# Output projection as one level of Strassen over pairs of token tiles, and split sums of squares

## The reference, cut to what matters

```
mod = silu(c) W_ada + b_ada -> (shift, scale, gate)
h   = rms_norm(x, g_pre) * (1 + scale) + shift
proj = h W_in                       # 1024 x 6144: q f i hg | dq dk dv dg | ma mb
o_a = hgrn2 recurrence over f, q, i (4 heads of 128), per-head rms_norm, * silu(hg)
o_b = differential attention (4 heads of 128, two maps), per-head rms_norm, * silu(dg)
y   = sigmoid(ma) * (o_a W_a) + sigmoid(mb) * (o_b W_b)
y   = y W_out                       # 1024 x 1024, "output projection"
out = x + gate * rms_norm(y, g_post)
```

## Time and profile before

| | |
|---|---|
| three runs, median | 907.11 us (904.93 to 907.34) |
| profiled execution | 902.09 us |
| its span, first to last instruction | 900.3 us |
| TensorE (PE) busy | 852.6 us, 95% |
| DVE / ACT / POOL busy | 567.0 / 450.0 / 446.2 us |
| share of PE in the chain that ended last | 80% |
| mean granted TensorE clock | 0.990 of full speed |

### The profile page before, as it was taken

One profiled execution on the slowest core, in us unless ns is written; L12 is line 12 of the kernel. 1 busy time (PEld: TensorE's weight loads), 2 busy tenths in 40 slices (PEclk: granted clock), 3 DMA queues, 4 the chain that ended last, 5 costly groups with the idle time before them and its releaser, 6 DMA issues.

```text
span 900.3 us, 12969 instructions
## 1 busy us (share of the span) xinstructions
PE 852.6 (95%) x4829; PEld 671.8 (75%) x4829; DVE 567.0 (63%) x682; ACT 450.0 (50%) x826; POOL 446.2 (50%) x336
## 2 busy tenths in 40 slices
PE   2899899999999999999999999999999999899996
PEld 2677677777777777777777777778788888678885
DVE  4889984788694897866887948746200622872222
ACT  7686222885345875336864436754445731421111
POOL 6065665455554445653554645567788461830000
PEclk9899899999999999999999999999999999999998
DMA  9914221102110120121021011102221741111331
GB/s 328 332 44 146 71 71 47 48 1 71 48 48 24 48 71 1 48 71 42 6 72 48 13 59 48 61 11 67 86 60 48 280 148 40 35 59 47 107 104 70
DMA packets 74625, 68.10 MB, mean 76 GB/s; under 512 B 3716, under 2 KB 65220, under 8 KB 74564
## 3 DMA queue, kind: packets, MB, share of 16 engines
q1 hardware_dynamic: 74448, 67.25, 23.2%
q10 hardware_dynamic: 116, 0.03, 0.0%
HBM read 58.88 MB, written 8.39 MB: 75 GB/s over the span
## 4 chain that ended last, share of the span: by engine, by line
PE 80%; DVE 11%; issue 5%; ACT 2%; SPq 1%; DMA 1%; DVEq 0%; ACTq 0%
PE pj L890 14%; PE pj L892 13%; PE pj L891 13%; PE sp L955 8%; PE sp L710 4%; PE by L725 3%; PE by L751 2%; DVE acc L1403 2%; PE sp L927 2%; PE bx L719 2%; PE sp L929 2%; PE sp L928 2%; DVE k L1537 1%; DVE sc L1578 1%; DVE q L1536 1%
## 5 line engine op out<-in xcount | busy, mean ns | idle before, releaser
L599 POOL TENSOR_TENSOR w_lo<-w_raw,w_hi 128x512 fp32r<-128x512 f32 x140 | 193.3, 1382 | 255.6 <-ACT w_hi L1169 254.1
L890 PE MATMUL pj<-b_hi,w_hi 128*128 128x512 f32 x616 | 262.0, 425 | 4.6 <-DVE dk L1517 3.3
L892 PE MATMUL pj<-b_hi,w_lo 128*128 128x512 f32 x616 | 242.2, 393 | 0.0
L891 PE MATMUL pj<-b_lo,w_hi 128*128 128x512 f32 x616 | 241.8, 393 | 0.0
L890 PEld LDWEIGHTS pj<-b_hi,w_hi 128*128 128x128 f32 x616 | 116.4, 189 | 42.1 <-issue 9.0
L892 PEld LDWEIGHTS pj<-b_hi,w_lo 128*128 128x128 f32 x616 | 116.2, 189 | 26.2
L891 PEld LDWEIGHTS pj<-b_lo,w_hi 128*128 128x128 f32 x616 | 116.7, 190 | 21.9 <-issue 3.1
L1169 ACT ACTIVATE w_hi<-w_raw 128x512 fp32r<-128x512 f32 x132 | 82.8, 627 | 63.4 <-PE pj L892 57.4
L580 POOL TENSOR_TENSOR w_raw<-w_raw,w_raw 128x512 f32<-128x512 f32 x66 | 92.7, 1404 | 3.8 <-DMA w_raw<-in_w_in 0.9
L684 POOL TENSOR_TENSOR y2n<-y2n,res 128x512 f32<-128x512 f32 x1 | 1.3, 1260 | 96.6 <-DVE y2n L1752 96.6
L1184 ACT ACTIVATE p<-sp,cols 128x1024 f32<-128x1024 f32 (+7 forms) x64 | 46.9, 738 | 0.8
(11 more groups left out here) (274 smaller groups left out, 1777.8 us busy)
## 6 DMA issues: line engine op xcount, KB each, us to landing
w_raw<-in_w_in SPq DMA_DIRECT2D x96, 256.0 KB, 4.2
x_in<-in_x SPq DMA_DIRECT2D x8, 512.0 KB, 7.1
ada<-in_w_ada SPq DMA_DIRECT2D x16, 256.0 KB, 7.1
ada<-in_w_ada SPq DMA_DIRECT2D x8, 512.0 KB, 8.1
ada_g<-in_w_ada SPq DMA_DIRECT2D x8, 512.0 KB, 3.9
wo_raw<-in_w_out SPq DMA_DIRECT2D x8, 512.0 KB, 4.2
res<-in_x SPq DMA_DIRECT2D x8, 512.0 KB, 4.1
out_x<-y2n SPq DMA_DIRECT2D x7, 512.0 KB, 2.9
```

The source lines that it names most:

```text
L599: pool.tensor_tensor(w_lo[slot(v)][:, :], raw[:, :], w_hi[slot(v)][:, :].bitcast(F32), ALU.subtract).then_inc(s_wlo, 1)
L890: pe.matmul(bank[:, :], wh, part(b_hi[m], kk), start=(fresh and kk == 0), stop=False, skip_group_check=True)
L891: pe.matmul(bank[:, :], wh, part(b_lo[m], kk), start=False, stop=False, skip_group_check=True)
L892: last = pe.matmul(bank[:, :], wl, part(b_hi[m], kk), start=False, stop=(kk == 3), skip_group_check=True)
```

## The change

**Output projection.** W_out is cut into four quarters, y into blocks of 512 rows by 128 tokens. Token tiles t and t+4 form a pair, and each of the four pairs is one more Strassen group (products `STEPS` to `END`), run by the same `product`, `snap` and `event` code and the same `pj` banks and `w_hi`/`w_lo` ring: 7 x 12 = 84 matmuls a pair where two tiles took 96. The y blocks take the place of the weights, so ACT writes a hi (`y_high`) and POOL a lo (`low_y`) for every product, and POOL makes five sums a pair (`combine_y`). The seven combinations of W_out (128x2048 each) are made by DVE (`combine_w`), split by ACT (`sum_high`) and DVE (`low_w`): those of M1, M5, M6 and M2 in the branch stage, those of M7, M3 and M4 after it. `wo_hi`, `wo_lo`, `y_hi` and `y_lo` of before are gone. Results go to SBUF (`rows_o`), one tile pair at a time; ACT squares them there, and DVE scales and adds there (`finish_o`).

**Sums of squares.** After the square ACT writes its rounded part (`hi_a`, `hi_b`) and DVE the remainder (`lo_a` in slots 60 and 61, `lo_b` in slots 33 and 48); the ones are rounded too (`ones_r`); TensorE adds two fp32r matmuls instead of one float32 one.

```diff
+LOWB_AT, LOWA_AT = (33, 48), (60, 61)
...
             sp_.wait_ge(s_olo[0], HEADS)
+            load_wo(0, b_raw[M1], 0, 0)
             for m in range(2, 2 * KT):
                 load_wb(m)
...
+            def low_y(v, raw):
+                ring_free(v)
+                pool.wait_ge(s_whj, act_highs(v) + 1)
+                pool.tensor_tensor(in_four(w_lo[slot(v)][:, :]), raw, in_four(w_hi[slot(v)][:, :].bitcast(F32)),
+                                   ALU.subtract).then_inc(s_wlo, 1)
...
+            first_sum_y(0)
+            for t in range(PAIRS_OUT):
+                a11, a12, a21, a22 = [y_tile(j, kh, t) for j in range(2) for kh in range(2)]
+                v = use(STEPS + PROD * t)
+                low_y(v + M1, a11)
+                low_y(v + M2, a12)
+                if t == 0:
+                    second_sum_y(0)
+                pool.wait_ge(s_wlo, v + M6)
+                combine_y(a11, s2, a11, ALU.add)
+                low_y(v + M6, s2)
+                combine_y(a12, a12, a22, ALU.subtract)
+                low_y(v + M5, a11)
+                low_y(v + M7, a21)
+                combine_y(a12, a12, a21, ALU.add)
+                low_y(v + M3, a12)
+                low_y(v + M4, a22)
+                if t + 1 < PAIRS_OUT:
+                    first_sum_y(t + 1)
+                    second_sum_y(t + 1)
...
                 elif name == "ssa":
-                    pe.wait_ge(s_sqa, 2 * h + n + 1)
-                    last = pe.matmul(by[:, :], ones[:, :], k[:, n * HALF:(n + 1) * HALF], start=True, stop=True)
+                    pe.wait_ge(s_loa, 2 * h + n + 1)
+                    pe.wait_ge(s_ones, 1)
+                    pe.matmul(by[:, :], ones_r[:, :], hi_a[n][:, :], start=True, stop=False)
+                    last = pe.matmul(by[:, :], ones_r[:, :], lo_a[n][:, :], start=False, stop=True)
                 elif name == "ssb":
-                    pe.wait_ge(s_sqb, 2 * h + n + 1)
...
+                    pe.wait_ge(s_lob, 2 * h + n + 1)
+                    pe.matmul(bx[:, :], ones_r[:, :], hi_b[n][:, :], start=True, stop=False)
+                    last = pe.matmul(bx[:, :], ones_r[:, :], lo_b[n][:, :], start=False, stop=True)
...
-            for t in range(NT - 1):
-                if t >= 2:
-                    pe.wait_ge(s_y2f, t - 1)
...
+            for n in range(STEPS, END):
+                for half in range(2):
+                    product(n, half)
...
                     act.activation(part(k, e), part(k, e), ACT.Square, scale=DOWN).then_inc(s_sqa, 1)
+                    act.wait_ge(s_sqa, 2 * h + e + 1)
+                    act.wait_ge(s_unit["o"], 2 * h + 2)
+                    act.activation(hi_a[e][:, :], part(k, e), ACT.Copy).then_inc(s_hia, 1)
...
+                for h, e in attention(m, LOWB_AT):
+                    dve.wait_ge(s_hib, 2 * h + e + 1)
+                    dve.tensor_tensor(lo_b[e][:, :], (sig, p1)[e][:, 0:HALF], hi_b[e][:, :].bitcast(F32),
+                                      ALU.subtract).then_inc(s_lob, 1)
...
+            def finish_o(i):
+                t, j = divmod(i, 2)
+                o = rows_o[t % 2][j][:, :]
+                norm_o(i)
+                dve.scalar_tensor_tensor(out=o, in0=o, scalar=r_o[:, i:i + 1], in1=gp_row[:, :],
+                                         op0=ALU.mult, op1=ALU.mult).then_inc(s_y2f, 1)
+                dve.wait_ge(s_y2f, i + 1)
+                dve.wait_ge(s_xr[i % 4], 16 * (i // 4 + 1))
+                dve.tensor_tensor(o, o, res[i % 4][:, :], ALU.add).then_inc(s_fin, 1)
+
+            dve.wait_ge(s_unit["br"], 4 * KT)
+            combine_w(M7, wo_22, wo_12, s_t3)
+            low_w(M3, wo_22, 1)
+            for n in range(STEPS + 1, END):
+                t, x = divmod(n - STEPS, PROD)
+                event(n - 1)
+                if t == 0 and x == 2:
+                    dve.wait_ge(s_t3, 2)
+                    low_w(M7, b_raw[M7], 2)
+                    low_w(M4, b_raw[M4], 2)
+                if t and x == 1:
+                    finish_o(2 * t - 1)
+                if x == PROD - 1:
+                    finish_o(2 * t)
...
```

More of the change, by code:

```diff
@@ L393, in build @@
         s_ysum = sem("s_ysum")
[L394 to L398, removed]
+        s_wo = [sem(f"s_wo{n}") for n in range(4)]
         s_agl = [sem(f"s_agl{n}") for n in range(4)]
@@ L409, in build @@
         s_y2f = sem("s_y2f")
-        s_xr = [sem(f"s_xr{n}") for n in range(2)]
+        s_xr = [sem(f"s_xr{n}") for n in range(4)]
         s_fin, s_finp = sem("s_fin"), sem("s_finp")
@@ L1721, in _ @@
                     dve.wait_ge(s_bro, n + 1)
[L1722 to L1729 removed]
+                    dve.tensor_tensor(part(sb[m], half), part(y[m], half), part(sb[m], half), ALU.add).then_inc(s_ysum, 1)
+                if n == 6:
+                    dve.wait_ge(s_olo[1], HEADS)
+                    dve.wait_ge(s_wo[0], 16)
+                    dve.wait_ge(s_wo[1], 16)
+                    combine_w(M5, wo_12, b_raw[M1], s_t1)
@@ L1749, in _ @@
-            norm_o(NT - 1)
-            dve.wait_ge(s_out[1], 16 * (NT // 2 - 1))
-            for n in range(2):
-                dve.scalar_tensor_tensor(out=part(y2n[1], n), in0=sp[:, 1, n * HALF:(n + 1) * HALF],
-                                         scalar=r_o[:, NT - 1:NT], in1=part(gp_row, n), op0=ALU.mult,
-                                         op1=ALU.mult).then_inc(s_y2f, 1)
+                    dve.wait_ge(s_y2s, i + 1)
+                then(dve.tensor_scalar(ss_o[:, i:i + 1], ss_o[:, i:i + 1], RS / D, EPS * RS, ALU.mult, ALU.add))
@@ L1755, in _ @@
+            norm_o(NT - 1)
+            last = rows_o[1][1]
+            for n, src in enumerate((pj[(END - 1) % 2][:, :], part(last, 1))):
+                dve.scalar_tensor_tensor(out=part(last, n), in0=src, scalar=r_o[:, NT - 1:NT], in1=part(gp_row, n),
+                                         op0=ALU.mult, op1=ALU.mult).then_inc(s_y2f, 1)
             dve.wait_ge(s_y2f, NT + 1)
-            dve.wait_ge(s_xr[1], 16 * NT // 2)
-            dve.tensor_tensor(part(y2n[1], 1), part(y2n[1], 1), part(res[1], 1), ALU.add).then_inc(s_fin, 1)
+            dve.wait_ge(s_xr[3], 32)
@@ L1760 @@
+            dve.tensor_tensor(part(last, 1), part(last, 1), part(res[3], 1), ALU.add).then_inc(s_fin, 1)
 _INS = ["x", "c", "w_ada", "b_ada", "g_pre", "g_post", "w_in", "lb_logits", "hg_norm_gain", "lambda_q1", "lambda_k1",
```

310 lines of the change are left out of this document (187 added, 123 removed).

## The result

The changed kernel is slower: 924.91 us median (919.68 to 927.00) against 906.02 us (901.99 to 907.34), ratio 1.0215 with a 95% interval of 1.0185 to 1.0245. The prediction was 910.8, with a range up to 917: the direction was right, the size was not. The profiled execution took 919.68 us with a span of 917.7, 17.4 us more than the span of 900.3 before.

The account below looks back on a forecast made before the run. TensorE was taken to bound the kernel. Sums of squares +7.8, branch stage -5.0, output stage -1.0 and tail +1.9 gave +3.7 us on a median of 907.1, so 910.8 us; range 901.5 to 917.

Parts of the forecast that it names:

- What bounds the kernel: Whole kernel: TensorE, 80% of the chain; every microsecond of it saved or stalled counts nearly in full.
- Savings on TensorE, -10.9 and -6.5: Output projection 336 matmuls instead of 384, 10.9 us less; sixteen sums of squares 0.41 each, 6.5 us, if all stayed fed.
- Sums of squares, +7.8: Rounds: TensorE waits for remainders in DVE's order, +7.8 us where 6.5 was to be gained; bounds +4 to +12.
- The first `ssb`: Rounds 1 to 3: remainder behind L1581, 1.35 us late, 0.41 saved, +0.94 each, +2.8 in all.
- The second `ssb`: Rounds 1 to 3: remainder behind L1581 delays matmul and `kt`, +1.2 us each, +3.7 in all.
- a rival of 0.12: Rival: POOL gets in first, sums of squares +12 instead of +7.8, total +7.9, 915.0 us; chance 0.12.
- `ssa` and transposes: Each head: first `ssa` +0.13, second -0.2, delayed softmax work holds transposes 0.6 us; +0.5 a head, +2.1 for four.
- The lock: DVE and POOL exclude each other: each two-input SBUF operation of DVE adds some 1.0 us per 1024 elements to POOL.
- Branch stage, -5.0: Branch stage: 5.5 us of TensorE stalls shrink to 0.5, so -5.0; bounds -5.5 to 0.
- Output stage, -1.0: Output projection: POOL and DVE work adds up, last M4 ready at 83.3, done at 86.0 against 87.05; bounds -3.3 to +2.
- Tail, +1.9: After the last matmul: last tile's scaling waits behind tile 6, +1.9 us; bounds +1 to +2.5.
- Signs: Observations to confirm: `ssb` gaps about 1.3 and 2.2 us, first seven output products over 24, POOL nearly without idle time.

Follow-up runs that it names:

- all remainders moved: Changed kernel with ssb remainders moved to DVE slots 31 and 47, second ssa remainder to 62, ssa matmuls to 62 and 64; 901.98 us, ratio 0.9989.
- the one with float32 sums: Changed kernel with sums of squares as before (one float32 matmul each, no rounded copy or remainder), only the output projection changed; 902.48 us, ratio 0.9991.
- rounded squares: Changed kernel with squares rounded in place by ACT, remainder left out, one fp32r matmul per sum; 897.99 us, ratio 0.9929.
- DVE's sums with the late finishing: Changed kernel with float32 sums of squares, y-block sums on DVE instead of POOL, odd tile's finishing behind M2's event; 894.73 us, ratio 0.9905.
- that with the split: Changed kernel with y-block sums on DVE, odd tile's finishing behind M2's event, split sums of squares with ssb and ssa remainders moved; 895.89 us, ratio 0.9907.
- the kernel with DVE's sums alone: Changed kernel with float32 sums of squares and the five y-block sums of each pair on DVE instead of POOL; 907.62 us, ratio 1.0040.

## Why the prediction was wrong, step by step

- **What bounds the kernel.** Half right: every wait of TensorE in the rounds counted in full. That every microsecond saved counts too did not hold in these slots: with all remainders moved, the 6.5 us saved came back as 6.9 us of waits for DVE's copy and ACT's exponentials.
- **Savings on TensorE, -10.9 and -6.5.** Right in size: a pair runs in 19.04 us when fed.
- **Sums of squares, +7.8. This step failed, by 10.9 us.** Its mechanism, remainders late by their place in DVE's list, was right: with all of them moved, the kernel keeps pace with the one with float32 sums from 160 to 650 us to within 0.1 us. Three sizes were off. (1) The first `ssb`: +3.1 against +2.8, right. (2) The second `ssb`: +9.4 against +3.7. In two of three heads POOL's operation got in first (+1.1 each), which I had priced as a rival of 0.12; and I left the clock out: after an idle time of 3.25 us it was at its lower level, 1.57 us each time. The rest is 0.15 a head. (3) `ssa` and transposes: +7.0 against +2.1. The first half came out at +0.55 a head instead of +0.13: from the end of DVE's remainder to the matmul are 0.15 to 0.29 us, where I had put 0.05, and ACT's copy was 0.1 later. The second half with the transposes is +1.12 instead of +0.4, for I took 0.6 of a span of 0.3 to 1.2 where it is the upper end. The reason is in the working: I delayed one instruction by 2.3 us and asked what it would be late for, but not what it would now meet. It met POOL. My upper bound was also added up wrongly: 7.8 + 3 x 1.2 for POOL and 4 x 0.6 for the transposes is +13.8, not +12, which would have put that rival at 916.8 us; and it held no effect of the idle time.
- **The lock.** Right: 1.23 became 2.20 for 1024, as estimated; the additions of x and the scaling cost POOL 4.3 us a pair.
- **Branch stage, -5.0.** Right in kind, and just beyond its bound of -5.5: -5.7, no stall is left; the savings come where y_lo had stood, 1.4 us at a time.
- **Output stage, -1.0. Failed by 3.3 us.** The sum over POOL was right to half a microsecond: the last M4's remainder was forecast for +83.3 and ended at 902.62, +83.8. But it was the wrong instruction to end the sum with. In pairs 2 to 4 the late one is M5 (896.98 in the last), and from its start TensorE still has four products to run, 4 x 2.72 + 0.2 = 11.1: 908.1. I had M4 run right after its remainder, which by these rows would have ended at 905.3. And the event of M2, behind a finishing in DVE's list, was a second bound that I had not looked for; in the last pair it is the one that M5 waits for, and moving it was worth 1.2 us.
- **Tail, +1.9.** Right: +2.2.
- **Signs.** The gap before the first `ssb` was 1.27 against 1.3; before the second 3.25, 2.12 and 3.25 against 2.2. Products 818.79 to 845.75 took 27 us against over 24. POOL was busy for 77.1 of 89.6 us; 5.5 of the rest lie behind its last remainder.

Open is what sets the order of POOL and DVE where they start 0.02 us apart. In the changed kernel it falls one way in heads 0 and 2 and the other in head 1 of the profiled execution; how often in its other runs isn't known. Nor was it tested that the two groups of runs of one kernel, some 5 us apart, come from such a collision in the first head. The traces point there: of the twelve profiled executions, four (rounded squares, all remainders moved, DVE's sums with the late finishing, and that with the split) have TensorE wait 2.96 us for DVE's event at 115 to 118 us, with the granted clock at its lower level for 3.4 us in the first and 10.2 us in the other three; in the eight others that wait is 0.65 to 0.98 us and the clock stays up.

## What to carry to other kernels

Where work is moved to an engine that is nearly full, add up not only when the new instruction can start, but which instructions of the engine that shares its port will start in that moment now: a delay moves all that follows into new company. Put such an instruction as early in the list as its input allows, not just ahead of its user, and put what frees a PSUM bank ahead of long work that nobody waits for. And when a chain of late inputs is summed up, end it with the one behind which the most work still has to run, not with the last.

## What the runs showed of the hardware

- A two-input DVE operation of 512 elements and a POOL operation of 1.26 us: 1.78 for DVE if POOL started 0.02 us earlier, 0.69 if DVE did, and then POOL's takes 1.82. The later one waits for nearly all that is left of the earlier. The Trainium skill says so in "SBUF — State Buffer", section "Who interferes with whom" (the shared port pair is an exclusive lock, and the order of issue decides who blocks). These rows agree on the order; the wait that they show is a little short of the whole, 1.09 of the 1.24 us that POOL still had to run and 0.56 of DVE's 0.67. In the prediction I had read 1.0 us per 1024 elements as a price that POOL pays for each DVE operation. POOL does pay it (4.27 us a pair for the four operations left out), but where DVE comes second DVE pays, and its operation can be the one that TensorE waits for.
- TensorE's granted clock was at 2.4 GHz after an idle time of 2.12 us and at 1.2 GHz after one of 3.25 us (mean 0.63 over the next 4 us), in the middle of a stretch that was otherwise busy. Between these lie, in the kernel with DVE's sums alone, 2.54 us with the clock still at 2.4 GHz behind it, and 2.66 and 2.71 us with 1.2 GHz behind them.
- A matmul that is made shorter (0.63 us, sixteen times) moved the end by 4.5 us of 10.1 in a kernel whose TensorE is busy for 97% of those rounds.
